# Both token halves of a GEMM tile interleaved on the tensor engine, two PSUM banks in turn, in a hybrid decoder layer

## The reference, cut to what matters

```python
p = rmsnorm(x) @ w_in                      # 2048 -> 5120, columns [u_A | v_A | B_gate | C_gate | x_B]
u, v = gelu(u_A), rmsnorm(gelu(v_A))
y_A = u * (tril(W_s[h]) @ v_chunk + b_s[h])          # 8 heads, chunks of 128 positions
y_B = B_gate * causal_dwconv3(C_gate * x_B)
x = x + concat(group_rmsnorm(y_A), group_rmsnorm(y_B)) @ w_out       # 2048 -> 2048
h = rmsnorm(x)
x = x + (silu(causal_dwconv3(h @ w_gate)) * (h @ w_up)) @ w_down     # 2048 -> 5632 -> 2048
y = rmsnorm(x)
```

## Time and profile before

| | |
|---|---|
| median of 3 executions | 2511.51 us (2509.65 to 2513.96) |
| profiled execution, span from the first to the last instruction | 2507.9 us |
| mean granted TensorE clock over the span | 0.992 |
| tensor engine busy | 2462.1 us, 98% |
| VectorE, ScalarE, GpSimd busy | 48%, 25%, 6% |
| matmul instructions | 18,473, of which 18,048 of the 288-column kind |

### The profile page before, as it was taken

One profiled execution on the slowest core, in us unless ns is written; L12 is line 12 of the kernel. 1 busy time (PEld: TensorE's weight loads), 2 busy tenths in 40 slices (PEclk: granted clock), 3 DMA queues, 4 the chain that ended last, 5 costly groups with the idle time before them and its releaser, 6 DMA issues.

```text
span 2507.9 us, 45612 instructions
## 1 busy us (share of the span) xinstructions
PE 2462.1 (98%) x18473; PEld 2452.1 (98%) x18473; DVE 1206.8 (48%) x1902; ACT 617.1 (25%) x738; POOL 160.2 (6%) x279
## 2 busy tenths in 40 slices
PE   6999999999999999999999999999999999999996
PEld 6999999999999999999999999999999999999996
DVE  6357644556224535455434444444544354454445
ACT  6224312113113322222212222122222211222224
POOL 3310000001221000000000000000000000000004
PEclk8999999999999999999999999999999999999998
DMA  5422222224222222223222222222232222222222
GB/s 153 159 84 71 69 85 85 83 85 151 83 79 73 84 80 81 84 84 92 75 84 84 84 84 81 80 80 82 78 97 78 76 84 84 84 84 84 84 85 84
DMA packets 326837, 219.17 MB, mean 87 GB/s; under 512 B 6804, under 2 KB 301839, under 8 KB 324992
## 3 DMA queue, kind: packets, MB, share of 16 engines
q1 hardware_dynamic: 324432, 203.98, 27.2%
q0 software_dynamic: 2352, 14.41, 1.6%
HBM read 208.19 MB, written 10.18 MB: 87 GB/s over the span
## 4 chain that ended last, share of the span: by engine, by line
PE 96%; ACT 1%; DVE 1%; POOL 0%; issue 0%; DMA 0%; POOLq 0%; SPq 0%; DVEq 0%; ACTq 0%
PE ps L1161 32%; PE ps L1163 31%; PE ps L1162 31%; DVE h_lo L797 0%; POOL acc L470 0%; ACT ps L540 0%; PE ps L1284 0%; ACT h_hi L512 0%; PE ps L1297 0%; DMA x_nat<-in_x_prompt_dram 0%; ACT X L520 0%; PE ps L1296 0%; ACT w_hi L491 0%; DVE rms L813 0%; PE ps L1276 0%
## 5 line engine op out<-in xcount | busy, mean ns | idle before, releaser
L1161 PE MATMUL ps<-h_hi,w_hi 128*128 128x288 f32 x4608 | 1362.2, 296 | 6.2 <-issue 4.9
L1163 PE MATMUL ps<-h_hi,w_lo 128*128 128x288 f32 x4608 | 1358.7, 295 | 0.0
L1162 PE MATMUL ps<-h_lo,w_hi 128*128 128x288 f32 x4608 | 1358.3, 295 | 0.0
L1161 PEld LDWEIGHTS ps<-h_hi,w_hi 128*128 128x128 f32 x4608 | 865.6, 188 | 8.4 <-issue 5.8
L1162 PEld LDWEIGHTS ps<-h_lo,w_hi 128*128 128x128 f32 x4608 | 865.7, 188 | 0.0
L1163 PEld LDWEIGHTS ps<-h_hi,w_lo 128*128 128x128 f32 x4608 | 865.7, 188 | 0.0
L771 DVE TENSOR_TENSOR w_lo<-raw,w_hi 128x1024 fp32r<-128x1024 f32 x376 | 460.5, 1248 | 305.7 <-ACT w_hi L491 305.6
L491 ACT ACTIVATE w_hi<-raw 128x1024 fp32r<-128x1024 f32 x376 | 384.2, 1050 | 489.9 <-PE ps L1163 474.5
L1161 PE MATMUL ps<-act_hi,w_hi 128*128 128x288 f32 x1408 | 418.4, 297 | 1.0 <-DVE scaled L781 1.0
L1163 PE MATMUL ps<-act_hi,w_lo 128*128 128x288 f32 x1408 | 415.0, 295 | 0.0
L1162 PE MATMUL ps<-act_lo,w_hi 128*128 128x288 f32 x1408 | 414.3, 294 | 0.0
(11 more groups left out here) (184 smaller groups left out, 921.6 us busy)
## 6 DMA issues: line engine op xcount, KB each, us to landing
raw<-in_w_gate_dram SPq DMA_DIRECT2D x88, 512.0 KB, 3.9
raw<-in_w_up_dram SPq DMA_DIRECT2D x88, 512.0 KB, 3.8
raw<-in_w_down_dram SPq DMA_DIRECT2D x88, 512.0 KB, 4.3
raw<-in_w_in_dram SPq DMA_DIRECT2D x80, 512.0 KB, 4.3
raw<-in_w_out_dram SPq DMA_DIRECT2D x32, 512.0 KB, 4.0
xT_scratch<-X POOLq DMA_DIRECT2D x1, 4608.0 KB, 18.5
X<-xT_scratch POOLq DMA_DIRECT2D x4, 1152.0 KB, 5.6
x_nat<-in_x_prompt_dram SPq DMA_DIRECT2D x4, 1024.0 KB, 8.6
```

The lines of the kernel that those rows point to most:

```text
L1161: te.matmul(out, whi, xhi, start=start, stop=False)
L1162: te.matmul(out, whi, xlo, start=False, stop=False)
L1163: return te.matmul(out, wlo, xhi, start=False, stop=stop)
```

## The change

In `gemm`, `gemm2_by_k` and `down_tile`, the two halves are no longer made one after the other. For each weight tile the order is: w_hi x x_hi for half 0 and half 1, w_hi x x_lo for both, w_lo x x_hi for both. Consecutive matmuls write to two banks in turn, and a weight tile is used up before the next is begun. The number of matmuls, their shapes, their operands and the order of accumulation within each bank stay as they are. `piece_done` comes after half of the tile and at its end, and the wait for the second piece comes at half of the tile instead of a quarter. The small pieces of other work stay at a quarter, a half and three quarters. The first tile of all keeps the old order, in `first_gemm`, as its second half's activations come later.

```diff
--- before.py
+++ after.py
@@ -1156,29 +1156,44 @@
         def _(pe):
             te = nc.tensor
 
-            def three(out, whi, wlo, xhi, xlo, start, stop):
-
-                te.matmul(out, whi, xhi, start=start, stop=False)
-                te.matmul(out, whi, xlo, start=False, stop=False)
-                return te.matmul(out, wlo, xhi, start=False, stop=stop)
+            def three_pairs(p, whi, wlo, xhi, xlo, start, stop):
+
+                for w, x, first, end in ((whi, xhi, start, False), (whi, xlo, False, False), (wlo, xhi, False, stop)):
+                    for half in range(2):
+                        last = te.matmul(pair(p, half), w, x[:, half * HALF:(half + 1) * HALF], start=first, stop=end)
+                return last
 
             def gemm(q, c, p, q1=None, mid=None, q3=None):
 
+
+                for s in range(2):
+                    pe.wait_ge(lo_ready, q + s + 1)
+                    for k in range(PK):
+                        kk = s * PK + k
+                        last = three_pairs(p, w_hi[:, (c + s) % 4, k, :], w_lo[:, (c + s) % 4, k, :],
+                                           h_hi[:, kk, :], h_lo[:, kk, :], kk == 0, kk == KT - 1)
+                        hook = (q1, q3)[s] if k == PK // 2 - 1 else mid if s == 0 and k == PK - 1 else None
+                        if k == PK - 1:
+                            last.then_inc(piece_done, 1)
+                        if hook is not None:
+                            hook()
+
+            def first_gemm(q, c, p, mid):
 
                 for half in range(2):
                     cols = slice(half * HALF, (half + 1) * HALF)
-                    for s in range(2):
-                        if half == 0:
+                    for kk in range(KT):
+                        s, k = kk // PK, kk % PK
+                        if half == 0 and k == 0:
                             pe.wait_ge(lo_ready, q + s + 1)
-                        for k in range(PK):
-                            kk = s * PK + k
-                            last = three(pair(p, half), w_hi[:, (c + s) % 4, k, :], w_lo[:, (c + s) % 4, k, :],
-                                         h_hi[:, kk, cols], h_lo[:, kk, cols], kk == 0, kk == KT - 1)
-                        if half == 1:
+                        w, lo = w_hi[:, c + s, k, :], w_lo[:, c + s, k, :]
+                        te.matmul(pair(p, half), w, h_hi[:, kk, cols], start=kk == 0, stop=False)
+                        te.matmul(pair(p, half), w, h_lo[:, kk, cols], start=False, stop=False)
+                        last = te.matmul(pair(p, half), lo, h_hi[:, kk, cols], start=False, stop=kk == KT - 1)
+                        if half == 1 and k == PK - 1:
                             last.then_inc(piece_done, 1)
-                        hook = (q1, mid, q3, None)[2 * half + s]
-                        if hook is not None:
-                            hook()
+                    if half == 0:
+                        mid()
 
             def gemm2_by_k(q, ready, after):
 
@@ -1190,10 +1205,8 @@
                         c = 2 * tile + s
                         if k == 0:
                             pe.wait_ge(lo_ready, q + c + 1)
-                        for half in range(2):
-                            cols = slice(half * HALF, (half + 1) * HALF)
-                            last = three(pair(tile, half), w_hi[:, c, k, :], w_lo[:, c, k, :],
-                                         h_hi[:, kk, cols], h_lo[:, kk, cols], kk == 0, kk == KT - 1)
+                        last = three_pairs(tile, w_hi[:, c, k, :], w_lo[:, c, k, :],
+                                           h_hi[:, kk, :], h_lo[:, kk, :], kk == 0, kk == KT - 1)
                         if k == PK - 1:
                             last.then_inc(piece_done, 1)
                     if kk in after:
@@ -1255,7 +1268,7 @@
             assert HALF <= 3 * P
             pe.wait_ge(xlo_pool, 2 * 3)
             pe.wait_ge(xlo_dve, 2 * 3)
-            gemm(0, 0, 0, mid=rest_of_x)
+            first_gemm(0, 0, 0, rest_of_x)
             pe.wait_ge(vec_ready, 3)
             gemm(2, 2, 1, q1=spread_x_ssq, q3=params_t)
             for t in (2, 3):
@@ -1364,11 +1377,9 @@
 
             def down_tile(slot, jj, p, ks=(0, 1)):
 
-                for half in range(2):
-                    cols = slice(half * HALF, (half + 1) * HALF)
-                    for k in ks:
-                        last = three(pair(p, half), w_hi[:, slot, 4 * k + jj, :], w_lo[:, slot, 4 * k + jj, :],
-                                     act_hi[:, k, cols], act_lo[:, k, cols], k == 0, k == 1)
+                for k in ks:
+                    last = three_pairs(p, w_hi[:, slot, 4 * k + jj, :], w_lo[:, slot, 4 * k + jj, :],
+                                       act_hi[:, k, :], act_lo[:, k, :], k == 0, k == 1)
                 if ks[-1] == 1:
                     last.then_inc(down_done, 1)
```

## The result

The kernel after takes 2522.98 us (median of 4, 2521.91 to 2524.03), the one before 2511.10 us (median of 4). The ratio is 1.0044, with a 95% interval of 1.003 to 1.0058: slower by 12 us. The forecast was 2525 us. The profiled execution took 2523.55 us, 1.65 us more than its span.

A forecast was written before the change was run, and what follows sets the result against it. The tensor engine, busy 98% of the span, was taken as the bound. Gemm 11.1, down tiles 2.3 and last ones 0.1 us make 13.5; 2507.9 + 13.5 = 2521.4, plus 3.6 outside the span, 2525 us; range 2495 to 2545.

The forecast's parts named there:

- Forecast A: gemm and down tiles: mixed halves run at 133.3 ns a matmul, +13.5 us, 2525 us; chance 0.43.
- The waits: Weight slots released earlier, second piece needed later, VectorE reading after the tile's end: each worth 0.
- B: Every change of bank costs by itself, 1.6 to 2.5 ns in gemm: 27 to 43 us, 2539 to 2555; chance 0.16.
- C: No change: each matmul keeps its own half's pitch, 131.7 or 133.3 ns; 2510 to 2512 us; chance 0.21.
- D: Alternating banks relieves the bank: 16 us less, 2495 us, or 2287 with the whole surplus gone; chance 0.18.
- E: Alternation makes the tensor engine's clock fall for a tenth of the time, some +240 us; chance 0.02.
- The surplus is a tenth of the columns: Matmul stream runs at nine tenths of the clock: surplus 22 ns on 512 columns, 12.5 on 288, 3 on 64.
- The load isn't the limit: Tensor engine: transposes loading 128 columns of weights each follow at 110 ns, below the matmul pitch of 132.5.
- The gain of half 0 is lost when the halves mix: Half 0's 131.7 ns in long runs becomes 133.3 when halves mix; 0.83 ns on 13,344 gemm matmuls, 11.1 us.

The follow-up runs named there:

- the short loads: Kernel after, with the w_hi x x_lo matmuls loading and writing 72 of 128 weight columns in all tiles but the first: 2487.7 us, before 2512.8.
- undone gemm: Kernel after with gemm alone back in the order of before: median 2501.5 us against 2512.5 for before, ratio 0.997.
- the run with the columns in turn: Order of after, but all matmuls of a pair except half 1's last write the even bank while column halves alternate: 2522.6 us, before 2513.2.

## Why the prediction was right, and where its reasons were not

**The size and its place: right.** Forecast A was 133.3 ns for each matmul in mixed halves, 12.80 us a gemm tile, 25.60 us for 16 down tiles, gemm2_by_k unchanged, 13.5 us in all. The trace has those three tile times exactly. The parts of the 14.0 us: 2.9 in the 40 tiles of w_in, 1.1 in w_out, 21 x 0.43 = 9.0 in the FFN blocks, 1.1 around the second gemm2_by_k, where the clock was down once. The medians differ by 11.9 us. Without the stretch at the lower clock the 14.0 would be some 12.7 (that gemm2_by_k took 28.35 us, 27.02 in before). The forecast added 3.6 us for the time outside the span, which is 1.6 to 1.7 us in every execution of after; some 2 us of the 3.6 came from a profiled execution of before that was shorter than the median one. With 1.6 the sum gives 2523.0, the measured median; that close is luck, as single executions of after spread over 2.1 us.

**The waits: right.** Earlier release of the weight slots and the later need of the second piece were worth nothing, and VectorE's reads follow the end of the tile as before.

**Rivals.** B, a price per change, fell with the tile of after, 12.80 us and not 12.87 or more, and with the run lengths: 8 changes a tile cost nothing. C, each matmul keeps the pitch of its half, would have left the tile at 12.72 us. D, relief by the second bank: banks in turn over one range of columns gave 12.64 us, which is half 0's rate in one bank already; the bank has no part in it. The 122.5 ns beside D is a figure that its source (the Trainium skill, TensorE: Matmul & The Clock Gate, Back-to-back issue gap) calls that of an isolated matmul, not of a stream with a weight load for each, as here; the lowest steady pitch of 288 columns in these runs was 130.0 ns. E, the clock: 1.00 in the interleaved stretches but for 3 us. The profile of before has a granted clock of 1.00 at the transposes of the earlier trace rows too, so these don't show the lower level; those between 15.5 and 18.8 us do, at 0.50, and follow at the same 213 ns.

**"The surplus is a tenth of the columns": wrong.** The prediction read this from three widths, two of which are pairs of matmuls with other operands. The widths 256, 320 and 384 show a constant 13.3 ns a matmul. That the load of 128 float32 weights, which runs beside the stream, takes it is argued, not shown: every matmul has exactly one load, so a fixed cost of the matmul itself would look the same, and the short loads don't decide it. For the load speaks that moving the weights alone swaps the rates of the halves, which shows that at least those 1.7 ns hang on load and stream together. "The load isn't the limit" was true (at 192 columns the pitch stays at 111 ns; 288 are above it), but not being the limit isn't costing nothing, and the prediction set the load aside by that step. For 288 columns nine tenths of the clock give 120 / 0.9 = 133.3 ns, the same as 120 + 13.3, so the wrong reading had no price here; the forecast's figure came from the earlier trace rows. At 384 columns it would have said 177.8 ns, where 173.3 were measured. The 22 ns on 512 columns in the earlier trace rows fit the tenth and not the 13.3; they are pairs only, and no run here looked at them.

**"The gain of half 0 is lost when the halves mix": half right.** It is lost in gemm, in gemm2_by_k and in after's down tiles. But the down tiles behind an undone gemm mix the halves on every matmul and run at 130.0 ns, faster than half 0 ever did in before. So do four gemm tiles of the run with the columns in turn. Mixing isn't the cause by itself; it is one of the things that decide which of a few steady rates the matmuls keep. The prediction held because nearly all of after's interleaved matmuls follow interleaved matmuls or a wait, and fell into 133.3. What chooses the rate stays open. If all gemm tiles could be held at 130.0, as those four were, it would be 13,344 x 2.5 = 33 us; no run tried it.

## What to carry to other kernels

When the tensor engine is busy all the time, work out its pitch by stage, to a tenth of a ns, over long runs of one kind: the price of a new order stood in a stretch of the old trace that already half had it. Before calling a surplus per column or per instruction, vary the columns and the load separately. Changing a kernel in one stage can change the rate of the next with no edit there, so time the parts of a change also one without the other: here the new order in the down tiles and gemm2_by_k alone is 0.3% faster than the kernel before, where the whole change is 0.4% slower.

## What the runs showed of the hardware that was not expected

- Matmuls in fp32r with a hidden load of 128 weight columns each follow 13.3 ns later than 2.4 columns per ns would have it, for 256, 320 and 384 columns alike. That it is the load that takes them isn't shown.
- Depending on the address of the weights relative to that of the columns, 288-column matmuls in long runs over one range of columns lose 11.7 or 13.3 ns; moving the weights by 128 bytes swapped the halves' rates, moving everything did nothing.
- The same 192 matmuls ran at 130.0 or 133.3 ns each, depending on what ran before them, and stayed there over all of them. In one run four gemm tiles in a row were at 130.0 and the later ones, in the same order, at 133.3.
- The PSUM bank, changed on every matmul or never, had no effect on the time of a gemm tile of w_out: 12.64 us over half 0's columns and 12.80 us over both in turn.
